# Decoder step with paged latent attention: cached keys turned on VectorE, scores on 32x32 tiles of the array

## The reference, cut to what matters

```python
def mla_sample_attention(q_nope, q_rope, c_kv, k_rope, ckv_past, krope_past, w_uk, w_uv):
    scale = (MLA_NOPE + MLA_ROPE) ** -0.5
    q_lat = jnp.einsum('bthn,lhn->bthl', q_nope, w_uk)                # 8 samples, 8 heads, 256
    s_past = (jnp.einsum('bthl,bpl->bhtp', q_lat, ckv_past)           # 8192 x 256 per sample
              + jnp.einsum('bthr,bpr->bhtp', q_rope, krope_past))     # 8192 x 32 per sample
    ...
    p = jax.nn.softmax(s, axis=-1).astype(c_kv.dtype)
    lat = (jnp.einsum('bhtp,bpl->bthl', p[..., :P], ckv_past)
           + jnp.einsum('bhts,bsl->bthl', p[..., P:], c_kv))
    return jnp.einsum('bthl,lhv->bthv', lat, w_uv)
```

## Time and profile before

| | |
|---|---|
| time, median of 3 runs | 2272.66 us (2267.74 to 2276.37) |
| span of the profiled execution, first to last instruction | 2286.1 us |
| time of the profiled execution beside its span | not given by itself; its span is 13.4 us above the median |
| PE / PEld / DVE / ACT / POOL busy | 90% / 79% / 56% / 21% / 22% of the span |
| paged stage, first to last scores | 806.95 to 1137.33 us |
| first product of the output projection | 1172.4 us |

### The profile page before, as it was taken

The page is one execution under the profiler, slowest core; times in us unless marked ns, Lnnn a source line. Parts: engine busy times, 40 slices in busy tenths (PEclk is TensorE's granted clock), DMA queues, the critical chain, the costliest instruction groups (busy, mean ns, idle before and its releaser), DMA issues.

```text
span 2286.1 us, 33122 instructions
## 1 busy us (share of the span) xinstructions
PE 2047.2 (90%) x14222; PEld 1796.6 (79%) x14222; DVE 1281.6 (56%) x1551; ACT 482.7 (21%) x881; POOL 505.7 (22%) x395
## 2 busy tenths in 40 slices
PE   6977786798899988888879887999999999999988
PEld 6966574497567766666679874899999999999988
DVE  6776656338466543443444336468728738477464
ACT  4110011012454333333321214210000000000013
POOL 2312121022100111111113240133233333332311
PEclk8988787698799999999979999899999999999999
DMA  4102101011200165665401243111121121111202
GB/s 130 46 11 56 38 19 43 11 29 36 68 1 1 58 233 209 228 228 208 167 10 38 65 138 101 36 48 47 35 58 47 35 58 38 56 47 33 60 26 88
DMA packets 157262, 165.02 MB, mean 72 GB/s; under 512 B 18486, under 2 KB 143436, under 8 KB 152988
## 3 DMA queue, kind: packets, MB, share of 16 engines
q1 hardware_dynamic: 142538, 82.70, 12.6%
q0 software_dynamic: 7168, 75.50, 8.8%
q10 hardware_dynamic: 7412, 4.71, 0.7%
HBM read 153.95 MB, written 9.03 MB: 71 GB/s over the span
## 4 chain that ended last, share of the span: by engine, by line
PE 71%; DVE 20%; ACT 6%; issue 2%; DMA 0%; SPq 0%; ACTq 0%; DVEq 0%
PE PS L681 15%; PE PS L682 15%; PE PS L683 15%; PE PS L698 8%; DVE cu L1904 3%; PE PS L869 3%; PE PS L939 3%; PE PS L920 2%; PE PS L849 2%; DVE Sst L1555 2%; DVE ct L1890 1%; PE PS L924 1%; ACT Ps L1298 1%; DVE dsm L1752 1%; PE PS L739 1%
## 5 line engine op out<-in xcount | busy, mean ns | idle before, releaser
L611 POOL CAST whi<-wraw 128x1024 fp32r<-128x1024 f32 (+4 forms) x146 | 128.7, 881 | 1235.3 <-PE PS L683 1130.8
L681 PE MATMUL PS<-BH,whi 128*128 128x344 f32 x1152 | 370.2, 321 | 3.5 <-ACT RB L1121 3.5
L682 PE MATMUL PS<-BL,whi 128*128 128x344 f32 x1152 | 369.1, 320 | 0.0
L683 PE MATMUL PS<-BH,wlo 128*128 128x344 f32 x1152 | 368.8, 320 | 0.0
L613 POOL TENSOR_TENSOR wlo<-wraw,whi 128x1024 fp32r<-128x1024 f32 (+4 forms) x146 | 292.6, 2004 | 11.7
L681 PEld LDWEIGHTS PS<-BH,whi 128*128 128x128 f32 x1152 | 218.0, 189 | 4.0 <-ACT RB L1121 4.0
L682 PEld LDWEIGHTS PS<-BL,whi 128*128 128x128 f32 x1152 | 218.0, 189 | 0.0
L683 PEld LDWEIGHTS PS<-BH,wlo 128*128 128x128 f32 x1152 | 217.9, 189 | 0.0
L681 PE MATMUL PS<-XH,whi 128*128 128x344 f32 x528 | 178.4, 338 | 27.6 <-DVE Sst L1555 17.9
L1812 DVE TENSOR_TENSOR XT<-PS,XT 128x1032 f32<-128x1032 f32 x56 | 69.0, 1233 | 206.9 <-PE PS L683 206.7
L682 PE MATMUL PS<-XL,whi 128*128 128x344 f32 x528 | 175.5, 332 | 0.0
(11 more groups left out here) (383 smaller groups left out, 3863.4 us busy)
## 6 DMA issues: line engine op xcount, KB each, us to landing
wraw<-in_w_up_dram SPq DMA_DIRECT2D x44, 512.0 KB, 3.8
wraw<-in_w_in_dram SPq DMA_DIRECT2D x21, 512.0 KB, 4.1
wraw<-in_w_down_dram SPq DMA_DIRECT2D x24, 256.0 KB, 2.7
wraw<-in_w_down_dram SPq DMA_DIRECT2D x16, 320.0 KB, 3.2
xstage<-in_x_prompt_dram SPq DMA_DIRECT2D x8, 512.0 KB, 6.2
wraw<-in_w_out_dram SPq DMA_DIRECT2D x8, 512.0 KB, 3.9
sV<-in_cache_mem_v_dram SPq DMA_DIRECT2D x8, 512.0 KB, 5.6
sK<-in_cache_mem_k_dram SPq DMA_DIRECT2D x8, 512.0 KB, 3.9
```

Source lines behind the costliest of these rows:

```text
L611: gp.tensor_copy(hi, raw).then_inc(w_hi_done, 1)
L681: pe.matmul(out, wh[:, t, 0:m], hi[:, tile(t), s], start=(t == first), stop=False)
L682: pe.matmul(out, wh[:, t, 0:m], lo[:, tile(t), s], start=False, stop=False)
L683: ins = pe.matmul(out, wl[:, t, 0:m], hi[:, tile(t), s], start=False, stop=(t == last))
```

## The change

Keys are no longer turned by TensorE. VectorE transposes them block by block (32x32) from SBUF to SBUF: `turn_key_pair(g, n)` turns 64 of the 256 latent columns of all 16 rows (128 x 1024) into one of five slots of `KPT`, and `turn_rope_keys(g)` turns `rk` (128 x 512) into one of two slots of `KRT`. A block keeps its 32 partitions, so the contraction is over 32 rows at a time, and the scores are products with K = 32, M = 8, N = 128, each on its own 32x32 tile of the array: tile (r, j) reads partitions 32r and writes partitions 32j of bank r. The queries are repeated for the four row strips (`qr`, `qlatR`). Per group there are 9 rounds of 16 products, accumulated in banks 0 to 3; the four banks are one group's scores, with one set of banks for all groups.

The order changes with it. TensorE does, per group, `turn_weights(g)` and then `group_scores(g + 1)`, with `group_values(g)` inside it after the fifth of the nine rounds. The maximum and exp read four banks. `PTs` has two buffers and is copied out by ScalarE. The gathers have four buffers. The sum over a sample's four groups (`sequence_values`: one multiplication over 128 x 1024, additions over 128 x 512 and 128 x 256) goes to GpSimd, between two gathers, and stays on VectorE for the last sample. `KPT` and `KRT` lie over the weight ring, so SP's loads of `out` 0 and 1 wait for the last scores, and GpSimd splits them behind all gathers.

The core of the diff (left out: the new addresses, the semaphores' names, the waits of `copy_out`):

```diff
+            if j in (job_no[("out", 0)], job_no[("out", 1)]):
+                full(sp, ("ps", GT - 1))
...
+        def sequence_values(eng, step, b):
+
+            eng.wait_ge(seq_wd, b + 1)
+            emptied(eng, ("go", NG * b + NG - 1))
+            step(eng.tensor_tensor(Og[:, :, :], Og[:, :, :], wgt.unsqueeze(2).broadcast_to([P, NG, KVL]), ALU.mult))
+            step(eng.tensor_tensor(Og[:, 0:2, :], Og[:, 0:2, :], Og[:, 2:4, :], ALU.add))
+            eng.tensor_tensor(Oacc[:, b, :], Og[:, 0, :], Og[:, 1, :], ALU.add).then_inc(seq_o, 1)
...
-                full(gp, ("go", g - 3) if g >= 3 else ("po", NT - 1, H // 2 - 1))
+                full(gp, ("go", g - 4) if g >= 4 else ("po", NT - 1, H // 2 - 1))
...
-                split_weight(j)
-                if j == job_no[("out", 1)]:
+                if j == job_no[("out", 0)]:
                     for g in range(GT):
                         load_pages(g)
+                        if g >= NG and g % NG == NG - 1:
+                            sequence_values(gp, step, g // NG - 1)
+                split_weight(j)
...
-            def turn_keys(g, first, last):
-                s = g % 3
-                pe.wait_ge(page_in[s], 32 * (g // 3 + 1))
-                for j in range(first, last):
-                    for c in range(KV):
-                        turn(("kt", g, j, c), [rc[s][:, 4 * j + n, c * P:c * P + P] for n in range(4)])
-                if last == 4:
-                    turn(("krt", g), [rk[s][:, 4 * j:4 * j + 4, :].rearrange("p t r -> p (t r)") for j in range(4)])
-
             def group_scores(g):
-
-                key, b = ("gs", g), g // NG
+                key = ("ps", g)
                 begin(key)
-                for j in range(4):
-                    for c in range(KV):
-                        emptied(pe, ("kt", g, j, c))
-                emptied(pe, ("krt", g))
-                k = uses[key][1][0]
-                for c in range(KV):
+                b, kr = g // NG, KRT[:, g % 2, :]
+
+                def tiles(query, keys, **kw):
                     for j in range(4):
-                        pe.matmul(PS[32 * j:32 * j + 32, k, :], qlat[:, c, b, :], KT[:, j, c, :], start=(c == 0), stop=False,
-                                  skip_group_check=True)
+                        for r in range(4):
+                            q4 = slice(32 * r, 32 * r + 32)
+                            ins = pe.matmul(PS[32 * j:32 * j + H, r, 0:P], query[q4, :], keys[q4, j * P:j * P + P], skip_group_check=True,
+                                            tile_position=(32 * r, 32 * j), **kw)
+                    return ins
+
+                pe.wait_ge(kr_turned, g + 1)
+                tiles(qr[:, b, :], kr, start=True, stop=False)
                 for n in range(4):
-                    for j in range(4):
-                        ins = pe.matmul(PS[32 * j:32 * j + 32, k, n * P:n * P + P], qrz[:, b, n, :], KRT[:, j, :], start=False,
-                                        stop=(n == 3), skip_group_check=True)
+                    pe.wait_ge(kp_turned, 4 * g + n + 1)
+                    kp = KPT[:, (4 * g + n) % KSLOTS, :]
+                    for l in range(2):
+                        ins = tiles(qlatR[:, 2 * n + l, b, :], kp[:, l * 512:l * 512 + 512], start=False, stop=(n == 3 and l == 1))
+                    if n < 3:
+                        ins.then_inc(kp_used, 1)
+                    if n == 1 and g:
+                        group_values(g - 1)
                 end(ins)
...
-            turn_keys(0, 0, 4)
-            emptied(pe, "qlat")
-            pe.wait_ge(qz_new, 1)
+            pe.wait_ge(part_zero, 1)
+            group_scores(0)
             for g in range(GT):
-                group_scores(g)
-                if g + 1 < GT:
-                    turn_keys(g + 1, 0, 3)
                 turn_weights(g)
                 if g + 1 < GT:
-                    turn_keys(g + 1, 3, 4)
-                group_values(g)
+                    group_scores(g + 1)
+            group_values(GT - 1)
...
-            def keys_out(g):
-                if g == 0:
-                    full(act, "qlat")
-                for j in range(4):
-                    copy_out(("kt", g, j, 0), KT[:, j, 0, :], bank(("kt", g, j, 0)))
-                copy_out(("krt", g), KRT[:, :, :].rearrange("p j k -> p (j k)"), bank(("krt", g)))
-
             def group_exp(g):
                 act.wait_ge(g_max, g + 1)
                 if g >= 2:
                     full(act, ("gpt", g - 2))
-                act.activation(Ps[g % 2][:, :], bank(("gs", g)), ACT.Exp, bias=nmax[:, g:g + 1], accum_out=lsum[:, g:g + 1])\
+                act.activation(Ps[g % 2][:, :].rearrange("p (t r c) -> p r t c", t=4, r=4),
+                               PS[:, 0:4, 0:P].rearrange("p r (t c) -> p r t c", t=4), ACT.Exp, bias=nmax[:, g:g + 1], accum_out=lsum[:, g:g + 1])\
                    .then_inc(freed["s"], 1)
...
-            keys_out(0)
+            group_exp(0)
             for g in range(GT):
-                group_exp(g)
-                if g >= NG and g % NG == 0:
-                    sequence_weights(g // NG - 1)
-                if g + 1 < GT:
-                    keys_out(g + 1)
+                full(act, ("gpt", g))
+                if g >= 2:
+                    full(act, ("go", g - 2))
+                copy_out(("gpt", g), PTs[g % 2][:, :, :].rearrange("p n k -> p (n k)"), bank(("gpt", g)))
                 if g % NG == 0 and g:
                     act.wait_ge(seq_o, g // NG)
                 copy_out(("go", g), Og[:, g % NG, :], bank(("go", g))[:, 0:KVL])
-            sequence_weights(NS - 1)
+                if g + 1 < GT:
+                    group_exp(g + 1)
+                    if g % NG == NG - 2:
+                        sequence_weights(g // NG)
...
-            step(ve.memset(qrz[:, :, :, :], 0.0))
-            for n in range(4):
-                ins = ve.tensor_copy(qrz[32 * n:32 * n + 32, :, n, 0:H], small[64:96, 24:88].rearrange("p (h b) -> p b h", h=H))
-            ve.memset(qlat[:, :, :, :], 0.0).then_inc(lat_zero, 1)
+            for r in range(4):
+                ve.tensor_copy(qr[32 * r:32 * r + 32, :, :], small[64:96, 24:88].rearrange("p (h b) -> p b h", h=H))
             ve.tensor_copy(krs0, small[96:P, 16:24]).then_inc(qz_new, 1)
             for n in (1, 3):
                 full(ve, ("wk", n))
                 take(ve.tensor_copy(wukT[0:NOPE, 2 * n:2 * n + 2, :].rearrange("p h l -> p (h l)"), bank(("wk", n))[0:NOPE, :]))
             full(ve, "qlat")
-            ve.wait_ge(lat_zero, 1)
-            take(ve.tensor_copy(qlat[:, :, :, 0:H], bank("qlat")[:, 0:P].rearrange("p (c h b) -> p c b h", c=KV, h=H)))
-
-            def keys_out(g, first, last):
-                for j in range(first, last):
-                    key = ("kt", g, j, 1)
-                    full(ve, key)
-                    take(ve.tensor_copy(KT[:, j, 1, :], bank(key)))
-
-            def sequence_sum(b):
-
-                ve.tensor_reduce(nmS[:, b:b + 1], nmax[:, NG * b:NG * b + NG], AX, ALU.min).then_inc(seq_w, 1)
+            for a in range(4):
+                for r in range(4):
+                    ve.tensor_copy(qlatR[32 * r:32 * r + 32, a::4, :, :],
+                                   bank("qlat")[32 * a:32 * a + 32, 0:P].rearrange("p (c h b) -> p c b h", c=KV, h=H))
+            take_now(ve.tensor_copy(qlat[:, :, :, :], bank("qlat")[:, 0:P].rearrange("p (c h b) -> p c b h", c=KV, h=H)))
+            emptied(ve, ("wk", 2))
+            ve.memset(PS[:, 0:4, 0:P], 0.0).then_inc(part_zero, 1)
+
+            def turn_rope_keys(g):
+                ve.wait_ge(page_in[g % 4], 32 * (g // 4 + 1))
+                if g >= 2:
+                    full(ve, ("ps", g - 2))
+                ve.transpose(KRT[:, g % 2, :], rk[g % 4][:, :, :].rearrange("p t r -> p (t r)")).then_inc(kr_turned, 1)
+
+            def turn_key_pair(g, n):
+                before = 4 * g + n - KSLOTS
+                if before >= 0:
+                    if before % 4 == 3:
+                        full(ve, ("ps", before // 4))
+                    else:
+                        ve.wait_ge(kp_used, 3 * (before // 4) + before % 4 + 1)
+                ve.transpose(KPT[:, (4 * g + n) % KSLOTS, :].rearrange("p (l t c) -> p l t c", l=2, t=GP),
+                             rc[g % 4][:, :, 64 * n:64 * n + 64].rearrange("p t (l c) -> p l t c", l=2)).then_inc(kp_turned, 1)
+
+            def group_max(g):
+                full(ve, ("ps", g))
+                ve.tensor_reduce(nmax[:, g:g + 1], PS[:, 0:4, 0:P], AXY, ALU.max, negate=True).then_inc(g_max, 1)
+                if g % NG == NG - 1:
+                    b = g // NG
+                    ve.wait_ge(g_max, g + 1)
+                    ve.tensor_reduce(nmS[:, b:b + 1], nmax[:, NG * b:NG * b + NG], AX, ALU.min).then_inc(seq_w, 1)
+
+            def sequence_total(b):
                 ve.wait_ge(seq_wd, b + 1)
```

(59 more changed lines are left out.)

49 lines of the change are left out of this document (24 added, 25 removed).

## The result

The changed kernel takes 2362.49 us (median of 4 runs, 2356.91 to 2366.55) against 2270.20 us before on the same chip: a ratio of 1.040, 95% interval 1.038 to 1.042. It is slower, and the forecast of 2198 us and its range were both wrong. The profiled execution has a span of 2364.5 us, 78 above that of before (another execution, on another chip; the kernel before takes 2270 to 2288 us from chip to chip, so the 78 of the two profiles and the 92 of the medians on one chip are not the same measure).

A forecast was written before the change was run, and what follows sets the result against it. TensorE was taken as the limit, key transposes about half its work. 31 steps of 8.21 us against 330.4 us before, -75.9, plus 1.1 for head and tail, gave 2198 us; range for 8 in 10: 2135 to 2285.

The forecast's parts named there:

- S: Score products of a group on TensorE: 288 records at 13.3 ns, 3.84 us a step, forecast's own range 2.5 to 5.5.
- values: Value products on TensorE, first to first: 1.75 us a step.
- `turn_weights`: Four weight transposes on TensorE at 0.11 us each: 0.44 us a step.
- latency and mode changes: TensorE step: 0.17 us for the last matmul's latency, 0.45 us for three changes of tile shape.
- the issue is the limit: Rival in `group_scores`: issuing small records limits, S 7.69 us, step 12.06 us, 2317 us in all; chance 0.14.
- The clock: TensorE in the stage: clock stays near 1.0; rival: falls to 1.2 GHz, step 10.6 us, 2272 us, chance 0.04.
- Maximum and exp exposed: TensorE stands still during each group's maximum, exp and hand-overs: 1.56 us a step.
- VectorE: VectorE's step: transposes cost like copies, 1.22 us per 1024 elements, 0.69 per 512; 6.4 us, below TensorE's 8.21.
- GpSimd and gathers: Gathers of 5.4 us per group and the sample sum of 4.2 us on GpSimd fit the step; nothing waits.
- Head: Before the stage: VectorE's query copies and first key turn make the first scores end later, +2.4 us.
- Tail: After the last scores: smaller `snew` and VectorE steps save 1.3 us; late loads of `out` weights stay hidden.

The follow-up runs named there:

- e5: Changed kernel with score products of K = 128 on block-diagonal queries (zeros outside each strip), 108 records a step: 2149.55 us, ratio 0.947 to the kernel before.
- e9: e5 with each score product cut in two (N = 64), 180 records a step: 2226.13 us.
- e8: e5 with each score product cut into four (N = 32), 324 records a step: 2349.40 us, ratio 1.035 to the kernel before.
- e6: e1 without gathers from the fifth group on: 2190.82 us.
- e2: Changed kernel with every score product cut to N = 32 of its 128 columns, same count of records: 2385.86 us.
- e12: Changed kernel with each gather issued later, after the exponential of group g - 3: 2366.95 us, ratio 1.034 to the kernel before.
- e1: Changed kernel with each score round as 4 products of N = 512 instead of 16 of N = 128, column-strip sums left out: 2296.31 us.
- e7: Changed kernel with one of two score rounds on each pair of turned blocks left out, 196 records a step: 2270.32 us.

## Why the prediction was wrong, step by step

The chain that ended last, 830 to 1130, by line:

```profile
by line: PE PS L920 39.0%; issue 22.9%; PE PS L948 22.4%; PE PS L709 5.5%; DVE dsm L1752 5.4%; ACT Ps L1296 4.9%
```

By these shares (a part of exp stands under "issue", so the pauses are taken from the waits), the 4.74 us by which the step was missed (12.95 against 8.21) are: pauses 2.73; scores 5.05 (39.0%) where S was 3.84, +1.21; values 2.90 (22.4%) where 1.75 stood, +1.15; `turn_weights` 0.71 for 0.44, +0.27; and the 0.62 for latency and mode changes isn't seen beside them, -0.62.

- **The scores, S.** This term failed, by a resource that it left out. The price from the earlier trace rows is right for what it measures: at 951.42, with the packet there, 96 score records open in 1.27 us, 13 ns each, and 12.0 over the best 120. But the earlier trace rows shows 12 instructions. 288 records with their loads are over two packets, and one comes in 5.0 us: 39 ns per record over a step, or 25 ns even at the least spacing seen. With the 2.04 us of pauses that stand before them, the scores take 7.1 us a step, above the 5.5 at which the forecast called itself wrong. The page of before listed a queue of instruction packets, and I did not set their number against the instructions that the change adds. As e5, e9 and e8 have it: no pause at 108 records in 6.0 us, 1.5 us of them at 180, 3.5 at 324.
- **Rival "the issue is the limit"** put the threshold at 21.8 ns per record and its own price at 26.7, and gave 2317 us. Its sign was right (no run tests the threshold), and the argument against it is what misled; its mechanism, a TensorE "running gapless but at low use", is not what happened, so that its 2317 us lie nearer to 2362 than the forecast is in part luck. At 0.14 its chance was too low.
- **The clock.** The forecast kept it near 1.0 by a stretch of 10 us with little work; it was 0.85. That stretch was a weak witness: in the kernel before, the clock fell to 0.5 at 1149.02 us, 1 us behind it, and stayed there until 1176.32. Values run at 3.57 us in a half-clock stretch. The rival had priced this (3.5 us) but saw its cause in thin use alone. What the runs show is that it mostly goes with standing still: e5 and e6 have no pause and 1.00, e2 with a quarter of the scores' columns and 3.8 us of pauses has 0.63. But it doesn't follow the length of the pauses alone: e12 has 1.9 us and 0.79, the changed kernel 2.7 us and 0.84. e1, which waits 3.6 us in one piece before it turns the weights, had 0.81 without any packet pause. Pauses and clock were not separated by a run, so the 2.73 is shown, and the 1.2 for scores and 1.15 for values are read from rows at either level.
- **Maximum and exp exposed**: right (TensorE idle 1.66 us, 23 times in 300 us, predicted 1.56).
- **VectorE**: right. Its transposes, which had no row, cost what a copy was reckoned at, 1.22 us (1203 ns here), and 669 ns for `KRT` (0.69):

```profile
L1747 DVE STREAM_TRANSPOSE KPT<-rc x128: 1200/1203/1236, 803.1 to 1206.4; 128x1024 f32<-128x1024 f32 x128
```

- **GpSimd and gathers**: nothing waits for a page, as said. That the issue of a gather may hold TensorE was not thought of; it cost the changed kernel little (its maximum starts 0.04 to 0.21 us late), but 0.6 us of each step of the kernel before from which I reckoned.
- **Head**: first exp 2.5 us later (+2.4 predicted), by luck. VectorE's copies began at 796.6 and not at 800, so the first group's keys were turned by 807.6 and not 811.2; then TensorE stood 2.81 us for a packet (begun at 807.99). **Tail**: from the last exp to the output projection 34.6 us where it was 31.5, +3.1 and not -1.3. `snew` shrank as reckoned (0.53 for 1.13), but the last sample's sum, which I had costed only on GpSimd, lies open on VectorE, and the last values ran at half clock (3.49 for 1.97):

```profile
1220.95 1.73 DVE L599 TENSOR_TENSOR Og<-Og,dsm 128x1024 f32<-128x1024 f32 x1 [5.03 <-ACT Og L1287]
1221.55 2.03 POOL L620 CAST whi<-wraw 128x1024 fp32r<-128x1024 f32 x1
...
1222.72 1.41 DVE L600 TENSOR_TENSOR Og<-Og 128x512 f32<-128x512 f32 x1
1223.66 2.66 POOL L622 TENSOR_TENSOR wlo<-wraw,whi 128x1024 fp32r<-128x1024 f32 x1
1224.16 2.44 DVE L601 TENSOR_TENSOR Oacc<-Og 128x256 f32<-128x256 f32 x1
```

The last addition, 256 elements, takes 2.44 us where the earlier trace rows gives 0.43, and it ends at 1226.60, 0.3 us after GpSimd's split of the weights, which this change moved beside it. The Trainium skill (SBUF — State Buffer, SBUF: two separate sides) says that a VectorE operation with two inputs in SBUF and a GpSimd operation that reads SBUF exclude each other for their whole length. The trace agrees.

## What to carry to other kernels

Count TensorE's instructions before splitting its work into small products. In this stage one packet of 128 matmuls with their loads per 6.9 us brought no pause; one per 6.4 us, in bursts, did (e7), and however short each product is, TensorE then stands still between packets, at a lower mean clock. Spend idle array rows instead (zeros on a block diagonal) to keep the count down; here that turned a change of +4.0% into one of -5.3% with the same transposes. Look also at what GpSimd issues beside the last product that another engine waits for, and have a buffer to spare before moving it.

## What the runs showed of the hardware that I had not expected

- **Instruction packets.** 256 instructions in 16 KB; beside gathers one in 4.8 to 5.3 us under full demand, without them in 3.9 to 4.0, never closer than 3.2, though a packet's own transfer takes mostly 0.9 to 1.2. TensorE goes on some 2.3 us after the packet began. Why the next one doesn't begin sooner is open. The Trainium skill (Runtime: NRT & Kernel Launch, Instruction fetch mechanics) says that the engine fetches the next 16 KB block while it executes the current one, and that crossing a block is mostly hidden, since dispatch is slower than the fetch. The block's size agrees (64 bytes an instruction, 16 KB a packet); the second half does not hold here: dispatch passes the 128 records of a packet in 1.7 us (13 ns each), and the next packet takes 4 to 5. The measurement decides.
- **Issue of gathers.** An indirect DMA issued on GpSimd (two of 0.95 us) delays the products beside it by 0.6 us (before: K = 128, 29 groups of 32) or 1.9 us (e1: K = 32, N = 512). In e2 TensorE opened 6 records and then none for 0.70 us, three times over. Such stops make up 1.6 us of e2's step. Why is open, and also why the changed kernel shows so little of it.
